# Spreading the gates of all experts in one pass, with half of them kept in HBM until their scores exist

## The reference, cut to what matters

```python
q = (xt @ w_pq).reshape(n_tok, PEER_HEADS, 2, PEER_HALF)          # 8 heads
v1, i1 = lax.top_k(s1, 16)                                        # s1, s2: scores against 128 sub-keys each
v2, i2 = lax.top_k(s2, 16)
sc, ic = lax.top_k(cand, 16)                                      # best 16 of the 16 x 16 sums
experts = (e1 * 128 + e2).reshape(n_tok, 128)                     # out of 16384
gate = jax.nn.softmax(sc, axis=-1).reshape(n_tok, 128)
act = gelu(einsum('tkd,td->tk', u_tab[experts], x))
y = einsum('tk,tkd->td', gate * act, v_tab[experts])
h = layer_norm(ALPHA * h + y)
```

## Time and profile before

| | |
|---|---|
| time, median of 3 runs | 1882.39 us (1881.47 to 1882.58) |
| time of the profiled execution | 1882.71 us |
| its span | 1880.9 us |
| PE busy | 1710.1 us (91%) |
| DVE busy | 1250.8 us (67%) |
| ACT busy | 204.6 us (11%) |
| POOL busy | 635.2 us (34%) |
| moved from HBM | 489.32 MB |

### The profile page before, as it was taken

The page is one execution under the profiler, slowest core; times in us unless marked ns, Lnnn a source line. Parts: engine busy times, 40 slices in busy tenths (PEclk is TensorE's granted clock), DMA queues, the critical chain, the costliest instruction groups (busy, mean ns, idle before and its releaser), DMA issues.

```text
span 1880.9 us, 19525 instructions
## 1 busy us (share of the span) xinstructions
PE 1710.1 (91%) x7236; PEld 1213.9 (65%) x7236; DVE 1250.8 (67%) x2616; ACT 204.6 (11%) x431; POOL 635.2 (34%) x536
## 2 busy tenths in 40 slices
PE   7999999989999799999728899999999958799996
PEld 6588878967555668888527666666666547544442
DVE  3343175122567669997888986777777699966664
ACT  1101033101111021112100000111011010000000
POOL 2000000000246200146550175765665661265340
PEclk9999999999999989999867799999999976799998
DMA  6715201954779635679992199999999991299994
GB/s 221 235 45 158 83 7 40 286 166 145 243 266 370 246 124 175 217 261 409 388 356 62 51 400 409 409 409 409 397 409 409 409 372 61 77 404 410 409 403 151
DMA packets 193834, 493.81 MB, mean 263 GB/s; under 512 B 14103, under 2 KB 92952, under 8 KB 193444
## 3 DMA queue, kind: packets, MB, share of 16 engines
q0 software_dynamic: 74672, 271.55, 37.6%
q1 hardware_dynamic: 119068, 221.01, 33.1%
HBM read 489.32 MB, written 7.90 MB: 264 GB/s over the span
## 4 chain that ended last, share of the span: by engine, by line
PE 43%; DVE 26%; DMA 14%; POOL 9%; issue 7%; ACT 0%; SPq 0%; DVEq 0%
PE ps L639 42%; DMA arena<-in_v_tab_dram,experts 10%; POOL arena L604 5%; DVE arena L1336 5%; POOL arena L613 4%; DVE arena L1303 2%; DVE arena L1314 2%; DMA arena<-in_v_tab_dram 2%; DVE i L1233 2%; DVE pos L1248 1%; DVE arena L1302 1%; DVE v L1232 1%; DVE best L1247 1%; PE ps L651 1%; DMA arena<-in_w_mem_kv_dram 1%
## 5 line engine op out<-in xcount | busy, mean ns | idle before, releaser
L639 PE MATMUL ps<-arena 128*128 128x256 f32 (+4 forms) x6016 | 1503.1, 412 | 75.8 <-ACT arena L887 23.1
L639 PEld LDWEIGHTS ps<-arena 128*128 128x128 f32 (+1 forms) x6016 | 1035.9, 188 | 537.9 <-issue 285.9
L604 POOL DMA_INDIRECT arena<-in_u_tab_dram,experts x256 | 326.6, 1276 | 860.5 <-DVE dots L1314 531.6
L1336 DVE SCALAR_TENSOR_TENSOR arena<-arena,coef 128x1024 f32<-128x1024 f32 x254 | 327.3, 1289 | 111.0 <-DMA arena<-in_v_tab_dram,experts 110.2
L1314 DVE CUSTOM_DVE_ANT_0 arena<-arena 128x1024 f32<-128x1024 f32 x256 | 312.4, 1224 | 87.9 <-DMA arena<-in_u_tab_dram,experts 87.7
L613 POOL DMA_INDIRECT arena<-in_v_tab_dram,experts x256 | 297.3, 1161 | 148.3 <-DVE arena L1336 97.7
L887 ACT ACTIVATE arena<-ps 128x256 f32<-128x256 f32 (+2 forms) x212 | 88.9, 427 | 765.7 <-PE ps L639 722.0
L639 PE MATMUL ps<-hotg,arena 128*128 128x64 f16 x512 | 68.1, 303 | 26.8 <-DVE hotg L1304 25.5
L639 PEld LDWEIGHTS ps<-hotg,arena 128*128 128x128 f16 x512 | 59.9, 147 | 34.7 <-DVE hotg L1304 34.7
L1198 DVE TENSOR_TENSOR arena<-arena,ps 128x128 f32<-128x128 f32 (+1 forms) x32 | 13.4, 418 | 103.0 <-PE ps L639 91.7
L887 ACT ACTIVATE arena<-ps,bT 128x128 f32<-128x128 f32 (+2 forms) x68 | 36.6, 538 | 313.5 <-PE ps L639 313.5
(11 more groups left out here) (127 smaller groups left out, 793.3 us busy)
## 6 DMA issues: line engine op xcount, KB each, us to landing
arena<-in_u_cols_dram SPq DMA_DIRECT2D x128, 512.0 KB, 6.8
arena<-in_v_tab_dram SPq DMA_DIRECT2D x128, 512.0 KB, 6.8
arena<-in_w_in_dram SPq DMA_DIRECT2D x37, 1024.0 KB, 5.6
arena<-in_w_o_dram SPq DMA_DIRECT2D x8, 1024.0 KB, 9.9
arena<-in_w_pq_dram SPq DMA_DIRECT2D x8, 1024.0 KB, 5.4
beta_copies<-beta_rows SPq DMA_DIRECT2D x1, 4608.0 KB
arena<-in_w_mem_kv_dram SPq DMA_DIRECT2D x4, 1024.0 KB, 18.6
arena<-in_w_a_dram SPq DMA_DIRECT2D x8, 512.0 KB, 6.2
```

The lines of the kernel that those rows point to most:

```text
L604: nc.gpsimd.indirect_dma_start(out=u_ring[:, n % ROWS, :], out_offset=None, in_=u_tab[0], in_offset=bass.IndirectOffsetOnAxis(ap=experts[: ...
L639: return nc.tensor.matmul(dst, lhsT, rhs, start=start, stop=stop, skip_group_check=True)
L1336: nc.vector.scalar_tensor_tensor(out=y_acc, in0=row, scalar=by, in1=y_acc, op0=ALU.mult, op1=ALU.add).then_inc(v_used, 1)
```

## The change

All gates are spread in one stage, before V0. `one_hots` and `scatter` work on all 128 slices of sub-key 1 at once, so a product has 128 columns where it had 64, and the result of a batch takes two banks, laid out as 4 tokens within each slice (a column step of 4 where it was 8). `take_spread` multiplies the first half into `acts` as before. A new ACT step, `spill`, copies the second half into SBUF after `take_spread` is done; every two batches SP writes it to HBM (`gates_kept`, 16 writes of 512 KB). There are three pairs of banks for the batches.

In stage V0, SP reads the kept gates back in 8 transfers of 1 MB (eight slices, 256 tokens, runs of 512 B), and DVE multiplies them into `acts` (`regate`) in 8 steps of 128 x 2048 elements, each placed `GATED_LAG = 4` slices behind the last slice that it needs. `V(64)` and each eighth slice after it wait for `regated`. Stage X1 is gone.

The factor `1 / GATE_UP` moves from `take_spread` to the last step, and `ALPHA * h` of the dense tiles to ACT. The pairs are dealt out anew: 34 where there were 42 in the last part of S0 (pairs up to 81), 4 in X0, 108 in V0 where there were 118, none in X1, and 87 in V1 where there were 65. The top 16 of step 7 are found after pair 76 where it was pair 86. The third buffer of `v_table` holds one of the `hotg` buffers during X0, so slice 2 of `v_tab` is loaded after it.

```diff
-REST_PAIRS = 42
-X_PAIRS = (4, 4)
-V_PAIRS = (118, PAIRS_IN - TAIL_PAIRS - TOP_PAIRS - REST_PAIRS - sum(X_PAIRS) - 118)
+REST_PAIRS = 34
+X_PAIRS = (4, 0)
+V_PAIRS = (108, PAIRS_IN - TAIL_PAIRS - TOP_PAIRS - REST_PAIRS - sum(X_PAIRS) - 108)
+KEPT = 2 * BT
+GRP = 8
+GATED_LAG = 4
+TOP_PAIR = {TOPK * (s - 2) + TOP_AT if s != HEADS - 1 else TOPK * (s - 2) - 4: s for s in range(2, GN)}
...
-            u.add(key, reader, bank=6 + key[2] % 2)
+            u.add(key, reader, bank=2 + 2 * (key[1] % 3), width=2)
...
-            for e in range(TAB_RING):
+            for e in range(TAB_RING - 1):
                 v_table(e)
             for e in range(TAB_RING, CW + TAB_RING):
                 u_table(e)
+            for q in range(GW // KEPT):
+                sp.wait_ge(spilled, (q + 1) * KEPT // BT)
+                sp.dma_start(gates_kept[q], kept[:, q % 2]).then_inc(gates_out[q % 2], 16)
+            wait_full(sp, ("X", BATCHES - 1))
+            v_table(TAB_RING - 1)
+
+            def gates_in(j):
+                if j >= 2:
+                    sp.wait_ge(regated, j - 1)
+                sp.dma_start(gates_back[j % 2].rearrange("p q e t -> p q (e t)"),
+                             gates_kept[:, :, j * GRP:(j + 1) * GRP, :].rearrange("q p e t -> p q (e t)")
+                             ).then_inc(gates_landed[j % 2], 16)
+
+            for j in range(2):
+                sp.wait_ge(gates_out[j], 16 * (GW // KEPT // 2))
             for e in range(TAB_RING, KEYS):
                 v_table(e)
                 if CW + e < KEYS:
                     u_table(CW + e)
+                if e < 2 + TAB_RING:
+                    gates_in(e - TAB_RING)
+                elif e % GRP == GRP - 1 and 2 * GRP < e < CW + 2:
+                    gates_in(e // GRP)
...
+            def scatter(b):
+
+                key = ("X", b)
+                pe.wait_ge(hot_ready, b + 1)
+                begin(key)
+                if b >= 3:
+                    pe.wait_ge(spilled, b - 2)
                 for t in range(BT):
+                    into = ps[:, units.bank[key] + t // 4, t % 4:4 * KEYS:4]
                     for i in range(2):
-                        last = mm(bank(key)[:, t:BT * CW:BT], hot2[:, n % 2, :, t], hotg[n % 2][:, i, :, t],
-                                  i == 0, i == 1)
+                        last = mm(into, hot2[:, b % 2, :, t], hotg[b % 2][:, i, :, t], i == 0, i == 1)
                 last.then_inc(full, 1)
...
+                if e == 0:
+                    wait_done(pe, ("X", BATCHES - 1))
+                    pe.wait_ge(spilled, BATCHES)
+                if e >= CW and e % GRP == 0:
+                    pe.wait_ge(regated, (e - CW) // GRP + 1)
...
+            def spill(b):
+
+                key, (q, i) = ("X", b), divmod(b, KEPT // BT)
+                wait_done(sca, key)
+                if q >= 2:
+                    sca.wait_ge(gates_out[q % 2], 16 * (q // 2))
+                bk = units.bank[key]
+                nc.scalar.activation(kept[:, q % 2, :, i * BT:(i + 1) * BT].rearrange("p e (k t) -> p k e t", k=2),
+                                     ps[:, bk:bk + 2, 4 * CW:8 * CW].rearrange("p k (e t) -> p k e t", t=4),
+                                     ACT.Copy).then_inc(spilled, 1)
...
+                c.link(nc.vector.tensor_tensor(hot1[:], iota_x[:], wide(keyT[:, 0, :]), ALU.is_equal))
+                nc.vector.tensor_tensor(hot2[:, b % 2], iota_x[:], wide(keyT[:, 1, :]), ALU.is_equal)
                 nc.vector.tensor_tensor(
-                    hotg[n % 2], hot1.unsqueeze(1).broadcast_to([P, 2, CW, BT]),
-                    gateT[:, :, toks].unsqueeze(2).broadcast_to([P, 2, CW, BT]), ALU.mult).then_inc(hot_ready, 1)
+                    hotg[b % 2], hot1[:].unsqueeze(1).broadcast_to([P, 2, KEYS, BT]),
+                    gateT[:, :, toks].unsqueeze(2).broadcast_to([P, 2, KEYS, BT]), ALU.mult).then_inc(hot_ready, 1)
...
+            def take_spread(b):
+
+                key = ("X", b)
                 wait_full(dve, key)
                 if b == 0:
+                    wait_done(dve, ("S", CW - 1))
+                mine = acts[:, :, b * BT:(b + 1) * BT].rearrange("p e (k t) -> p k e t", k=2)
+                bk = units.bank[key]
+                nc.vector.tensor_tensor(mine, ps[:, bk:bk + 2, 0:4 * CW].rearrange("p k (e t) -> p k e t", t=4),
+                                        mine, ALU.mult).then_inc(done, 1)
+
+            def regate(j):
+
+                wait_done(dve, ("S", CW + (j + 1) * GRP - 1))
+                dve.wait_ge(gates_landed[j % 2], 16 * (j // 2 + 1))
+                mine = acts[:, j * GRP:(j + 1) * GRP, :].rearrange("p e (q t) -> p q e t", t=KEPT)
+                nc.vector.tensor_tensor(mine, mine, gates_back[j % 2], ALU.mult).then_inc(regated, 1)
...
+            for i in range(CW + GATED_LAG):
+                if i < CW:
+                    pairs(v_pairs(0, i), v_pairs(0, i + 1))
+                if i >= GRP - 1 + GATED_LAG and (i - GATED_LAG) % GRP == GRP - 1:
+                    regate((i - GATED_LAG) // GRP)
+            pairs(v_pairs(1, 0), v_pairs(1, CW))
             gathered_norm(1)
             dve.wait_ge(vt_used, KEYS)
-            dve.wait_ge(h_in, 16)
+            dve.wait_ge(h_scaled, 1)
```

More of the change, by code:

```diff
@@ L181, in dense_units @@
             out += [(("ET", r), "dve") for r in range(GT)]
+    out += [(("X", b), "dve") for b in range(BATCHES)]
     for c in range(CHUNKS):
-        out += [(("X", c, b), "dve") for b in range(BATCHES)]
         for i in range(CW):
@@ L238, in plan @@
         u.add(key, reader)
-    u.before["y"] = {u.owner[b] for b in range(2, 6)} - {None}
     for key, reader in dense_units():
@@ L294, in build @@
     beta_copies = nc.dram_tensor("beta_copies", [DIL_HEADS * TABLES, P, DELTAS], F32).ap()
+    gates_kept = nc.dram_tensor("gates_kept", [GW // KEPT, P, CW, KEPT], F32).ap()
     h_kept = nc.dram_tensor("h_kept", [P, GT * D], F32).ap()
@@ L411, in build @@
         scaled = early[:, 256:512].rearrange("p (i t) -> p i t", i=2)
-        hotg_1 = sb("hotg_1", [P, 2, CW, BT], F16)
-        hotg = [hotg_0, hotg_1[:]]
+        hot1 = sb("hot1", [P, KEYS, BT], F16)
         ps = ctx.enter_context(nc.psum_tensor("ps", [P, BANKS, 512], F32))
@@ L439, in build @@
         act_ready = sem("act_ready")
-        h_out, h_in = sem("h_out"), sem("h_in")
+        spilled, gates_out = sem("spilled"), [sem(f"gates_out{j}") for j in range(2)]
+        gates_landed, regated = [sem(f"gates_landed{j}") for j in range(2)], sem("regated")
+        h_out, h_in, h_scaled = sem("h_out"), sem("h_in"), sem("h_scaled")
         out_ready, out_stored = sem("out_ready"), sem("out_stored")
@@ L868, in _ @@
                         tail_unit(("ET", r))
+            for b in range(BATCHES):
+                scatter(b)
             for c in range(CHUNKS):
-                for b in range(BATCHES):
-                    scatter(c, b)
-                if c == 0:
-                    for key in sorted(units.before["y"], key=lambda k: units.index[k]):
-                        wait_done(pe, key)
                 for i in range(CW):
@@ L999, in _ @@
             after_pairs(rest_pairs(CW), chunk_pairs(0))
+            for b in range(BATCHES):
+                spill(b)
+                after_pairs(x_pairs(0, b), x_pairs(0, b + 1))
             for c in range(CHUNKS):
-                for b in range(BATCHES):
-                    after_pairs(x_pairs(c, b), x_pairs(c, b + 1))
                 for i in range(CW):
@@ L1007, in _ @@
                 after_pairs(v_pairs(c, CW - ACT_LAG), v_pairs(c, CW))
+            sca.wait_ge(h_in, 16)
+            nc.scalar.activation(h_back, h_back, ACT.Copy, scale=ALPHA).then_inc(h_scaled, 1)
         @block.vector
@@ L1399, in _ @@
                 tail_unit(("ET", r))
-            for k in range(CHUNKS):
-                one_hots(k, 0)
-                for b in range(BATCHES):
-                    if b + 1 < BATCHES:
-                        one_hots(k, b + 1)
-                    take_spread(k, b)
-                    pairs(x_pairs(k, b), x_pairs(k, b + 1))
-                pairs(v_pairs(k, 0), v_pairs(k, CW))
+            one_hots(0)
+            for b in range(BATCHES):
+                if b + 1 < BATCHES:
+                    one_hots(b + 1)
+                take_spread(b)
+                pairs(x_pairs(0, b), x_pairs(0, b + 1))
+            for i in range(CW + GATED_LAG):
[4 more added lines that the diff above has]
+            pairs(v_pairs(1, 0), v_pairs(1, CW))
             gathered_norm(1)
             dve.wait_ge(vt_used, KEYS)
-            dve.wait_ge(h_in, 16)
+            dve.wait_ge(h_scaled, 1)
             for r in range(GT):
-                c.link(nc.vector.scalar_tensor_tensor(out=h_back[:, r, :], in0=h_back[:, r, :], scalar=ALPHA,
-                                                      in1=y_ps[:, r, :], op0=ALU.mult, op1=ALU.add))
```

(2 more changed lines are left out.)

45 lines of the change are left out of this document (14 added, 31 removed).

## The result

| | median us | runs |
|---|---|---|
| kernel before | 1882.08 | 4, 1881.47 to 1882.58 |
| kernel after | 1909.44 | 4, 1907.93 to 1909.86 |

What follows compares the result with a forecast made beforehand. The prediction took PE and DMA both to bound V0 and V1, and DVE narrowly X0. Its terms, 1073.0 + 744.1 + 24.8, gave a 1841.9 us span and 1843.4 us time, 2.1% less; 8-in-10 range 1820 to 1868.

Steps and rivals of the forecast that it cites:

- Step 1: End of S0: pairs 82 to 89 leave the stage, saving 29.3 us; PE's wait before ET falls to about 3.7 us.
- Step 2: X0: wider one-hots make DVE's batch 3.15 us, adding 24.9 us, plus 0.8 us for the last spill; V0 starts at 1073.0.
- I take the lower: X0: PE's 16 products with 128 columns keep their pitch, 2.14 us a batch, rather than rising to 3.9 us.
- PE limits the wide X0: Rival, 9%: in X0, PE's products take 4.1 us a batch, adding 29 us: 1873 us.
- Step 3: V0 start to last weigh: transfers set the length, 744.1 us, though PE's path is 104.4 us shorter.
- regate costs nothing as long as the rings keep DMA busy: V0 and V1: DVE needs some 531 of 744 us, so regate's 18.3 us are covered.
- margin of 42 us: V0: regate comes some 42 us after its read-back is issued, against 18 us for the slowest kind of landing.
- The sum: V0 start to last weigh: transfer terms add to 744.1 us, 28.8 of them for gates read back in 512 B runs.
- The slower rival: Rival, 5%: in V0, regate waits for gates and holds the gathers, losing 7.5 us eight times, 60 us: 1903 us.
- Step 4: Last weigh to the end of the span: the wait for PE goes, leaving 24.8 us of 43.0.
- three signs: Listed in advance: X0's 16 products over 3 us; V0 and V1 leaving 409 GB/s; idle time before regate.

Runs made afterwards that it cites:

- dense product: The kernel after with the scatter's moving operand read as 128 neighbouring elements instead of every eighth, for timing alone (gates wrong): 1883.63 us, one execution.
- dense output: The kernel after with the scatter's products written to neighbouring PSUM words instead of every fourth, for timing alone (gates misplaced): 1909.9 us, one execution.
- long runs: The kernel after with the gates grouped in HBM by their reader, so each read-back reads 8 KB in one run per partition: 1859.09 us.
- own queue: The kernel after with the read-backs issued by ACT on a queue of their own, still in runs of 512 B: 1871.67 us.
- late regate: The kernel after with regate ten slices behind the last slice it needs, where it was four: 1910.59 us.
- both cures: The kernel after with read-backs in 8 KB runs and the moving operand read in steps of 4 elements instead of 8: 1842.53 us.

## Why the prediction was wrong, point by point

**Step 1, the end of S0: right.** The shares are done at 950.4 (forecast about 952). PE's wait before ET is 17.4 and not 3.7 us, since the 10.3 us behind ACT vanished too and PE comes sooner; as the step says, nothing is gained or lost by it. Alone it is worth 19 us on the kernel before.

**Step 2, X0 gets wider: the failed term is "I take the lower" for PE's products.** I held that the pitch was set by weight loads and wouldn't move with columns, and left out the step at which the moving operand is read. For an operand without steps of 16 bytes the pitch indeed doesn't move: dense or in steps of 8 bytes, 128 columns take 0.12 to 0.13 us (1.97/16 and 2.14/16), as 64 columns did; that weight loads set it is not shown. In steps of 16 bytes, 128 columns take 0.236 us with the hand-overs (16.53/70), 1.84 ns a column. By that, 64 columns are 118 ns, no more than the 0.12 us that even the dense product takes: the trace of before couldn't tell the slow rate from the pitch I assumed. The batch is 3.75 us and not 3.15; thirty of them make 18 of the 19.4 us by which V0 started late. The rival "PE limits the wide X0" had the event and nearly the size (4.1 us), but gave PSUM's step as the reason. The products at half the time with that step kept refute it, and the dense output found nothing to gain at a clock of 0.50. DVE's prices were right within 20 ns.

The Trainium skill, "SBUF — State Buffer", section "Door 1: The DMA port swizzle", says that SBUF is read in lines of 16 bytes and that each line wants at least two hits. The moving operand agrees: one element of a line is slow (0.236 us a product), two of a line are nearly as fast as dense (2.14 against 1.97 us for 16). Its sentence on PSUM, which the prediction weighed, finds no support in the dense output's equal time, at a granted clock of 0.50. I read the half of that passage about the operand I had thought suspect.

**Step 3, V0 and V1 by their transfers: the failed step is "regate costs nothing as long as the rings keep DMA busy", with its margin of 42 us.** The margin was for the gates' landing against regate's slot. I listed what waits behind a regate on DVE, but not what stands behind a read-back in SP's queue: the slices that PE needs next. Moving the gates to a queue of their own recovers 41 of 46.5 us by the stretches (37.8 of 50.4 by the medians) at a landing of 40.7 us, which is within the margin as I'd reckoned it. The chain is: short runs, one packet a turn against the gathers' long packets; slices at 21 to 26 us; PE without v_tab; a late S; ACT and DVE in order behind it; no rows freed; no gathers. Each link has its row above, and the edits that break the first (long runs) or let the slices past it (own queue) remove the rest. The late regate shows that the last links don't depend on regate.

The Trainium skill, "DMA: Bandwidth & Descriptors", section "Queues, rings and completion order", says that each DMA engine goes round the queues that have work, packet by packet. The 4604 against 4832 packets of the two queues agree with it, if what the profile counts as a packet, here a single run, is what takes a turn. The section's own packet typically holds several descriptors, which no row here shows.

The sum itself held within 5 us or so. For the runs of 512 B that it prices, the stretch is 749.0 us with nothing behind them, against 744.1: the read-back costs 26.6 us (priced at 28.8), and the rest is 7 us short. That long runs come out at 743.6 and 741.3 us is partly luck, for by the same terms they would have 715.3 + 20.5 = 735.8. The stage start that goes, and both halves without a dip, are seen in the windows of the kernel with both cures.

**The slower rival** had what happens and when it decides (4.9 us a regate; it was 46/8 = 5.8), and put regate's own gates down as late. In fact 42.5 us of DVE's 133.7 are waits for gates; the rest is for S and act. At 5% it was far too cheap: its evidence was a margin that left out the queue.

**Step 4: right**, 24.7 us for 24.8. Of what would show each step wrong, three signs came: PE's 16 products over 3 us, GB/s below 409, and idle time before regate.

What stays open: whether the 5 to 13 us left of short runs in a queue of their own are their lower rate (by the earlier trace rows that would be 28.8 - 20.5 = 8.3 us) or the turns taken from the slices; which terms of the sum hold the missing 7 us; whether the threshold lies where DVE's slack ends; and what sets the 325 GB/s of the last 70 us.

## What to carry to other kernels

A new transfer is priced three times: its bytes, its runs, and what stands behind it in its queue; the last was about three quarters or more of the loss here, and another layout in HBM or another queue removes it. Before widening a matrix product, work out its time per column and ask what its operand's step is: the pitch of a narrow one may hide a slow reading. Where engines work in order, a late input can cost nothing up to the slack and then much at once, as it seemed to here (747.5 us at a landing of 19.3 us, 790.1 at 26.2), so test a suspected wait by moving the cause, not the instruction that waits.
